# Descending query tiles in the attention stage of a decoder step, with the sample's steps and cached values re-timed

## What is computed

```
y_ssd = rms_norm(y_ssd * silu(z), ssd_norm_g)              # 512 channels, every token

def prompt_attend(...):                                    # query tile i = 128 queries
    idx, valid = index_select(qi, wi, ki, q_pos, k_top)    # decided in an earlier stage
    return sparse_attend(q, k[idx], v[idx], valid)

def sparse_attend(q, ks, vs, valid):                       # 4 heads of 64 channels
    s = where(valid, q @ ks.T * 64**-0.5, -inf)
    return softmax(s) @ vs
```

## Time and profile before

| | us |
|---|---|
| runs | 3554.72, 3562.83, 3569.42; median 3562.83 |
| the profiled execution, whole | 3555.62 |
| its span in the trace | 3553.8 |
| TensorE busy | 3278.0 (92%) |
| attention stage, first and second layer, about | 175 each |

### The profile page before, as it was taken

How to read it: one execution, slowest core, us unless ns; L and a number is a source line. 1 busy time by engine, 2 the same in 40 slices (tenths; PEclk the granted TensorE clock), 3 DMA queues, 4 the chain that set the end, 5 groups by cost and what they waited for, 6 DMA issues and landing times.

```text
span 3553.8 us, 49876 instructions
## 1 busy us (share of the span) xinstructions
PE 3278.0 (92%) x19418; PEld 2659.8 (75%) x19418; DVE 1903.4 (54%) x3006; ACT 1217.4 (34%) x2262; POOL 663.4 (19%) x663
## 2 busy tenths in 40 slices
PE   7899899877999999999999999997788999999997
PEld 4454466545989999999854544765478999999996
DVE  5579783333664434435454996733247544335345
ACT  3256714234242222212233666241434312212123
POOL 0000000011033333334200000001110433334331
PEclk9899999768999999999989999995789999999998
DMA  4111114216011111111111010341340111111111
GB/s 135 45 30 36 34 41 138 87 54 181 8 36 47 35 57 36 48 48 39 64 45 47 30 40 25 97 120 44 116 127 1 45 51 36 51 51 33 57 33 69
DMA packets 168248, 205.77 MB, mean 58 GB/s; under 512 B 61185, under 2 KB 136258, under 8 KB 166850
## 3 DMA queue, kind: packets, MB, share of 16 engines
q1 hardware_dynamic: 163394, 201.43, 18.9%
q10 hardware_dynamic: 4608, 1.05, 0.1%
HBM read 189.33 MB, written 13.08 MB: 57 GB/s over the span
## 4 chain that ended last, share of the span: by engine, by line
PE 69%; DVE 13%; issue 9%; ACT 6%; SPq 1%; DMA 1%; ACTq 0%; POOL 0%; DVEq 0%; POOLq 0%; PEldq 0%
PE PS L785 44%; PE PS L766 5%; DVE MIX L1748 4%; PE PS L798 2%; PE PS L867 2%; ACT X L1388 2%; PE PS L995 1%; PE PS L1168 1%; DVE WORK L1937 1%; SPq L445 1%; PE PS L1145 1%; PE PS L960 1%; PE PS L1155 1%; ACT WORK L1553 1%; PE PS L1183 1%
## 5 line engine op out<-in xcount | busy, mean ns | idle before, releaser
L785 PE MATMUL PS<-WORK_parts,WHIGH_parts 128*128 128x352 f32 x3936 | 806.8, 325 | 19.6 <-DVE MIX_parts L2249 11.2
L785 PEld LDWEIGHTS PS<-WORK_parts,WHIGH_parts 128*128 128x128 f32 x3936 | 669.3, 190 | 23.2 <-issue 23.2
L785 PE MATMUL PS<-WORK_parts,RING_parts 128*128 128x352 f32 x3024 | 655.8, 325 | 0.0
L766 PE MATMUL PS<-X,RING 128*128 128x512 f32 (+1 forms) x1824 | 602.3, 493 | 22.5 <-ACT MIX L1457 9.6
L766 PEld LDWEIGHTS PS<-X,RING 128*128 128x128 f32 x1824 | 303.8, 193 | 321.2 <-issue 319.1
L785 PEld LDWEIGHTS PS<-WORK_parts,RING_parts 128*128 128x128 f32 x3024 | 520.4, 189 | 0.0
L1748 DVE SCALAR_TENSOR_TENSOR WORK<-WORK,VEC 128x1072 f32<-128x1072 f32 (+1 forms) x236 | 483.7, 2050 | 8.4
L509 POOL TENSOR_TENSOR RING_parts<-RING,WHIGH_parts 128x1024 fp32r<-128x1024 f32 (+2 forms) x184 | 373.1, 2028 | 446.5 <-ACT WHIGH_parts L1337 442.0
L1337 ACT ACTIVATE WORK<-PS 128x32 f32<-128x32 f32 (+11 forms) x412 | 190.8, 514 | 732.4 <-PE PS L785 565.2
L785 PE MATMUL PS<-X_parts,WHIGH_parts 128*128 128x352 f32 x2016 | 436.1, 324 | 0.0
L1746 DVE TENSOR_SCALAR WORK<-WORK,VEC 128x1072 f32<-128x1072 f32 (+1 forms) x90 | 70.6, 784 | 515.5 <-ACT WORK L1337 515.5
(11 more groups left out here) (335 smaller groups left out, 4021.4 us busy)
## 6 DMA issues: line engine op xcount, KB each, us to landing
RING<-w_up SPq DMA_DIRECT2D x88, 512.0 KB, 3.5
RING<-cache_k SPq DMA_DIRECT2D x256, 128.0 KB, 2.2
RING<-cache_v SPq DMA_DIRECT2D x256, 128.0 KB, 2.2
RING<-w_in SPq DMA_DIRECT2D x46, 512.0 KB, 3.6
RING<-w_down SPq DMA_DIRECT2D x80, 256.0 KB, 2.6
RING<-cache_kidx SPq DMA_DIRECT2D x192, 32.0 KB, 1.7
WORK<-w_out SPq DMA_DIRECT2D x12, 512.0 KB, 6.3
MIX<-xT SPq DMA_DIRECT2D x3, 1408.0 KB, 9.8
```

The costliest lines, as they stand in the source:

```text
L766: mm = pe.matmul(job_psum(n, w, first=first), stationary(k), moving(k)[:, first:first + w], start=k == 0, stop=k == k_tiles - 1)
L785: mm = pe.matmul(thirds(n)[:, third, :], a, x[:, third * THIRD:(third + 1) * THIRD], start=k == 0 and part == 0, stop=k == tiles - 1 and p ...
```

## The change

`BLOCKS` runs through the query tiles from 7 down to 0, so that the first eight pairs are the long ones. The other jobs get tables of their own: the samples' nine choices at pairs 0 and 1, all ten exponentials at pair 2, the nine transposes at pairs 3 and 4 between the pair's own steps; values from pair 5, two groups a pair up to pair 7 and three from pair 8; squares from pair 8, their sums at pairs 9 to 11, spread and scaling at 12 and 13 (in two parts through banks 3 and 1). A block is turned in pieces of up to four key tiles (`PIECES`), which alternate between banks 4 and 5. TensorE's iteration is now: turn the first block of pair p - 1, `scores(p)`, turn its second block, the other jobs, `weigh(p - 1)`. In the SSD stage the tick that needs bank 2 waits for `ssd["near_decay"]`, which rises after the fourth exponential of the chunk (the "half group").

```diff
-BLOCKS = [(i, h) for i in range(NCHUNK) for h in range(ATT_HEADS)]
-TURNED_AT, WEIGHED_AT = 4, 7
-
-
-def turns_of_pair(p):
-    return range(max(3 * (p - TURNED_AT), 0), min(max(3 * (p - TURNED_AT) + 3, 0), 9))
-
-
-def exps_of_pair(p):
-    return range(max(4 * (p - TURNED_AT + 1), 0), min(max(4 * (p - TURNED_AT + 1) + 4, 0), 2 * QUARTERS + QUADS))
+BLOCKS = [(i, h) for i in reversed(range(NCHUNK)) for h in range(ATT_HEADS)]
+
+
+CHOICES_OF_PAIR = {0: range(0, 5), 1: range(5, 2 * QUARTERS + 1)}
+EXPS_OF_PAIR = {2: range(2 * QUARTERS + QUADS)}
+TURNS_OF_PAIR = {3: range(0, 5), 4: range(5, 2 * QUARTERS + 1)}
+
+
+PIECES = [(_n, _s, min(_s + 4, BLOCKS[_n][0] + 1)) for _n in range(len(BLOCKS)) for _s in range(0, BLOCKS[_n][0] + 1, 4)]
+PIECES_OF = [[_q for _q, _piece in enumerate(PIECES) if _piece[0] == _n] for _n in range(len(BLOCKS))]
+PIECES_TO = [_of[-1] + 1 for _of in PIECES_OF]
 
 
 GATED = [(2 * _q, 2 * _q + 2) for _q in range(NCHUNK // 2)] + [(NCHUNK, NCHUNK + 1)]
-INVERTED_AT = len(GATED) + 1
-assert INVERTED_AT < NCHUNK - 1
+SQUARED_OF_PAIR = {8: (0, 1), 9: (2, 3), 10: (4,)}
+INVERTED_AT = 12
+WEIGHED_AT, VALUE_GROUPS = 5, [2, 2, 2] + [3] * 8 + [2]
+assert sum(VALUE_GROUPS) == STREAM
 
 
 def values_of_pair(p):
-    return range(max(3 * (p - WEIGHED_AT), 0), min(max(3 * (p - WEIGHED_AT) + 3, 0), STREAM))
+    n = p - WEIGHED_AT
+    if not 0 <= n < len(VALUE_GROUPS):
+        return range(0)
+    return range(sum(VALUE_GROUPS[:n]), sum(VALUE_GROUPS[:n + 1]))
...
+                    if q == 0:
+                        pool.wait_ge(att["out"], NCHUNK)
...
                 for n, (i, h) in enumerate(BLOCKS):
-                    if n % 2 == 0 and n // 2 < len(GATED):
-                        square_gated(n // 2)
                     pool.wait_ge(att["inverted"], n + 1)
                     s = SC[n % 4][:, 0:(i + 1) * P]
                     pool.tensor_scalar(s, s, RSUM[:, n:n + 1], 1.0, ALU.mult, ALU.mult).then_inc(att["normed"], 1)
+                    if n % 2:
+                        for q in SQUARED_OF_PAIR.get(n // 2, ()):
+                            square_gated(q)
...
                     if k % 8 == 1:
-                        pe.wait_ge(ssd["decay"], k // 8 + 1)
+                        pe.wait_ge(ssd["near_decay"], k // 8 + 1)
...
                 def scores(p):
 
-                    i, t = divmod(p, 2)
+                    i, t = BLOCKS[2 * p][0], p % 2
                     if p:
                         pe.wait_ge(att["masked"], 2 * p)
-                    if p == NCHUNK:
-                        pe.wait_ge(rms["scaled"], 1)
...
-                def turn_block(n):
-                    i, h = BLOCKS[n]
-                    pe.wait_ge(att["normed"], n + 1)
-                    if n >= 1:
-                        pe.wait_ge(att["copied"], n)
-                    for s in range(i + 1):
-                        mm = pe.transpose(bank(4 + s // 4)[:, (s % 4) * P:(s % 4 + 1) * P],
-                                          SC[n % 4][:, s * P:(s + 1) * P], c("ident"))
+                def turn_piece(q):
+                    n, first, end = PIECES[q]
+                    if first == 0:
+                        pe.wait_ge(att["normed"], n + 1)
+                    if q >= 2:
+                        pe.wait_ge(att["copied"], q - 1)
+                    for key in range(first, end):
+                        mm = pe.transpose(bank(4 + q % 2)[:, (key - first) * P:(key - first + 1) * P],
+                                          SC[n % 4][:, key * P:(key + 1) * P], c("ident"))
                     mm.then_inc(att["turned"], 1)
 
                 def weigh(p):
 
-                    i, t = divmod(p, 2)
-                    pe.wait_ge(att["copied"], 2 * p + 2)
-                    if t == 0 and i >= 1:
-                        pe.wait_ge(att["out_read"], i)
+                    i, t = BLOCKS[2 * p][0], p % 2
+                    pe.wait_ge(att["copied"], PIECES_TO[2 * p + 1])
+                    if t == 0 and p >= 2:
+                        pe.wait_ge(att["out_read"], p // 2)
...
+                    for ch in (4, 5, 6, 7) if again else (0, 1, 2, 3, NCHUNK):
...
-                def sample_steps(p):
-
-                    if 1 <= p <= len(GATED):
-                        yield lambda: sum_squares(p - 1)
-                    if p < TURNED_AT:
-                        for m in range(3 * p, min(3 * p + 3, 9)):
-                            yield lambda m=m: add_choice(m)
-                    for m in turns_of_pair(p):
+                def aside_steps(p):
+
+                    for q in SQUARED_OF_PAIR.get(p - 1, ()):
+                        yield lambda q=q: sum_squares(q)
+                    for m in CHOICES_OF_PAIR.get(p, ()):
+                        yield lambda m=m: add_choice(m)
+                    for m in TURNS_OF_PAIR.get(p, ()):
                         yield lambda m=m: turn_sample(m)
...
                 for p in range(n_pairs + 2):
-                    aside_steps = sample_steps(p)
+                    aside = list(aside_steps(p))
+                    turned = 1 <= p <= n_pairs
+                    if turned:
+                        for q in PIECES_OF[2 * p - 2]:
+                            turn_piece(q)
+                        if p in TURNS_OF_PAIR:
+                            aside.pop(0)()
                     if p < n_pairs:
                         scores(p)
-                    for now in list(aside_steps):
+                        if p in TURNS_OF_PAIR:
+                            aside.pop(0)()
+                    if turned:
+                        for q in PIECES_OF[2 * p - 1]:
+                            turn_piece(q)
+                    for now in aside:
                         now()
-                    if p == NCHUNK + 1:
-                        pe.wait_ge(rms["scaled"], 2)
-                    if 1 <= p <= n_pairs:
-                        turn_block(2 * p - 2)
-                        turn_block(2 * p - 1)
-                    if p == INVERTED_AT:
-                        spread_rstd()
-                    if p >= 2:
-                        weigh(p - 2)
+                    if p in (INVERTED_AT, INVERTED_AT + 1):
+                        spread_rstd(p > INVERTED_AT)
+                    if turned:
+                        weigh(p - 1)
...
+                        if h == 3:
+                            ins.then_inc(ssd["near_decay"], 1)
...
-                def copy_turned(n):
-                    i, h = BLOCKS[n]
-                    keys = (i + 1) * P
-                    act.wait_ge(att["turned"], n + 1)
-                    if n >= 4:
+                def copy_piece(q):
+                    n, first, end = PIECES[q]
+                    act.wait_ge(att["turned"], q + 1)
+                    if n >= 4 and first == 0:
                         act.wait_ge(att["out"], n // 2 - 1)
-                    copy(PROBT[:, h, 0:keys], bank(4, keys)).then_inc(att["copied"], 1)
+                    copy(PROBT[:, BLOCKS[n][1], first * P:end * P], bank(4 + q % 2, (end - first) * P)).then_inc(att["copied"], 1)
...
+                    samples_turned = list(TURNS_OF_PAIR.get(p, ()))
+                    if p >= 1:
+                        for n in (2 * p - 2, 2 * p - 1):
+                            for q in PIECES_OF[n]:
+                                copy_piece(q)
+                            if samples_turned:
+                                copy_sample(samples_turned.pop(0))
                     for n in (2 * p, 2 * p + 1):
                         if n < len(BLOCKS):
                             exp(n)
-                    for m in turns_of_pair(p):
+                            if samples_turned:
+                                copy_sample(samples_turned.pop(0))
+                    for m in samples_turned:
                         copy_sample(m)
-                    if p >= 1:
-                        copy_turned(2 * p - 2)
-                        copy_turned(2 * p - 1)
-                    for m in exps_of_pair(p):
+                    for m in EXPS_OF_PAIR.get(p, ()):
                         exp_sample(m)
-                    if p == len(GATED):
+                    if p == INVERTED_AT - 1:
...
-                for n in range(len(BLOCKS)):
-                    mask(n)
-                    if n % 2:
-                        invert(n - 1)
+                for p in range(len(BLOCKS) // 2):
+                    choices = list(CHOICES_OF_PAIR.get(p, ()))
+                    if p >= 3 and p % 2:
+                        take_out(BLOCKS[2 * p - 6][0])
+                    for n in (2 * p, 2 * p + 1):
+                        mask(n)
+                        if choices:
+                            add_choice(choices.pop(0))
+                    for n in (2 * p, 2 * p + 1):
                         invert(n)
-                    for m in range(3 * (n // 2) + 2 * (n % 2), min(3 * (n // 2) + 2 + n % 2, 9)):
+                        if choices:
```

(20 more changed lines are left out.)

30 lines of the change are left out of this document (17 added, 13 removed).

## The result

The changed kernel takes 3498.7 us (median of four runs, 3495.2 to 3503.6) where the kernel before takes 3561.8 beside it: ratio 0.982, 95% interval 0.981 to 0.984.

A forecast was written before the change was run, and what follows sets the result against it. The prediction took the stream of cached values to set the attention stage's end; attention -8.4 and SSD -4.4 us made -12.8 a layer, -25.6 in both, so 3537 us against a median of 3562.8, range 3514 to 3562.

The forecast's parts named there:

- What bounds the kernel: Attention stage: the stream of cached values sets the end; to gain, it must start earlier or run without holes.
- The stream of values: Attention from the first cached value: 10.7 us of SyncE's slot waits go, 1 and 5 come back; loading 78.2.
- The front: Attention stage up to the first cached value: 81.3 us becomes 77.5, first use 3.7 earlier.
- the wait of 3.96: Pair 3 of attention: TensorE waits about 4 us for ScalarE, which is busy with the samples' exponentials.
- third rival: Attention front: clock rises already in pair 0 and holds; -22.4 us a layer, 3518 in all; chance 0.18.
- 5 at the sums of squares: Pairs 9 and 10 of attention: loss taken as 5 us, between 1 at full clock and about 12 at half.
- second rival: Sums of squares in attention: clock falls and stays down, 12 us instead of 5, 3551 in all; chance 0.24.
- The end: Attention stage, from the last value load to the next stage: left at 10.0 us.
- The SSD stage: SSD stage: waiting for four exponentials instead of nine saves 0.55 us a chunk, -4.4 a layer, between 0 and 9.3.
- The wait that I priced: SSD stage: TensorE waits 1.17 us a chunk for the ninth exponential, 9.3 over eight chunks in the first layer.
- The rule against the change: Values beside short pairs: an engine waiting for loads between bursts falls back to the slow clock; would give 3551.

The follow-up runs named there:

- e5: The changed kernel with values begun one pair later (pair 6) and taken by threes; attention stage 160.1 and 159.9 us.
- e12: The changed kernel with half of the cached value loads left out and every matmul kept; attention stage 137.4 and 139.7 us.
- e16: The kernel before with three quarters of the sums of squares left out; first value at 70.8 and 73.4 us, attention stage 162.3 and 161.0.
- e15: The changed kernel with three quarters of the sums of squares left out; attention stage 150.7 and 151.2 us.
- e6: The changed kernel with each of the five sums of squares done twice; attention stage 167.6 and 169.8 us.
- e7: The changed kernel with matmuls that compute nothing behind the choices, ahead of late value groups and ahead of the last transposes; 3489.0 us, ratio 0.981.
- e4: The changed kernel with the samples' choice spread as in the kernel before and values from pair 7 in threes; 3481.6 us, ratio 0.981.
- e10: The changed kernel with blocks turned and copied whole, as before, instead of in pieces; 3502.8 us, ratio 0.984.
- e9: The kernel before with matmuls that compute nothing added in pairs 0 to 6; 3548.4 us, ratio 0.997.

## Why the prediction was wrong, step by step

**What bounds the kernel: right.** The stream of values sets the end (e5, e12), and it had to start earlier.

**The front: wrong in its size, 14 to 15 us and not 3.7.** This is the step that carried the miss out of the range, 10 to 11 us a layer. Pairs 0 to 4 and the lead of pair 5 were summed as 18 + 17 + 26 (pairs 2 and 3) + 11.5 and 5; in the first layer they took 14.2, 16.2, 24.4, 8.5 and 4.1. The mechanisms were there, the wait of 3.96 among them. In pair 0, 3.8 of the 10, the clock was set too low: I took the lower level for the whole pair and let it rise in pair 1; it was at 0.95 from 686 on, 2.6 us into the stage. Pair 4, 3.0 more, ran at 1.00; its term names no level. Idle time didn't shrink (15.0 before, 14.9 after), so what the front gained is busy time. How the remaining 3 us come about isn't shown. That the clock rises already in pair 0 is the first half of the third rival; its second half, that it holds, did not come. The rival was given 0.18 because choices leave gaps, and the clock did come down among them (0.50 from 694 to 698), but only behind the third choice.

A second reading would have warned me. Taking three quarters of the sums of squares out of the old front, and nothing else, brings 9.1 (e16), so all of them some 12, an estimate by proportion. A gain of 3.7 meant that the long pairs would eat two thirds of that.

**The stream of values: right as a sum, 78.2 against 76.3 and 78.6, by luck in its parts.** Beyond the 72.2 that SyncE needs unhindered, the forecast had 6, of them 5 at the sums of squares; the queue lost 4.1 and 6.4. But with a quarter of the sums it still loses 4.6 and 4.8 (76.8 and 77.0, e15), so it isn't the sums. The loss is spread: the longest group of four takes 3.86 and 4.30 us instead of 2.58. The second rival's mechanism exists: doubled, the sums bring the clock down and cost 15 (e6); as they are, it falls only behind them.

**The end: 10.0 forecast, 8.6 and 8.0 measured.** That less stands behind the last value, with the long pairs gone from it, is argued. A higher clock didn't shorten it (e7).

**The SSD stage: -4.4 forecast, -9.8 and -10.8 measured**, beyond the bound of 9.3 too. The wait that I priced came out about right: TensorE's waits for ScalarE at the turns fall from 9.3 us to 5.8 in the first layer, and its idle time by 2.1 and 2.0. What the sum put at nothing is the granted clock: 7.7 and 8.9 us of busy time went with it in these two executions. This is the second step that failed, 5 to 6 us a layer.

**The rule against the change.** The clock did fall among values beside short pairs: 0.50 in the last window, as the rule says (the Trainium skill, TensorE: Matmul & The Clock Gate, section "HAM oscillation — how this bites in real kernels"). It cost nothing that shows there: at 1.00 the end of the first layer was no shorter (e7).

**The samples' choice in the first pairs** was priced as part of the front's gain; e4 has the same front without it. Of the rest, the moved sums (e16) and the pieces (1 us, e10) are shown to give a part of it; the descending order and the weighing one pair sooner were not tried alone.

How the gain of the front divides exactly stays open: sums (12, estimated), clock (3.6 in e9, with the fills to pay for) and pieces (1) overlap, and the long pairs bring work of their own.

## What to carry to other kernels

When a wait of TensorE goes, price the granted clock of the stretch too: in the SSD stage 2 us less of idle time came with 8 us less of busy time at a higher clock. Read a cause off the sums of the whole stage and not off one chunk: the chunk shown loses a wait for keys, the stage doesn't. Check a sum built up from parts against what is taken out: if 15 us of work leaves the bounding engine and your sum gains 4, name what eats the rest. Try long, solid work around short steps that take turns with another engine (0.94 in e4's front against 0.54); and where a single queue's issue pace sets a stage, a second queue helps only if its engine reaches the issue in time.

## What was not expected of the hardware

- TensorE busy 5.00 of 5.00 us with matmuls of one column, each with its own weight load, is brought down to the lower clock (0.50, e6), where two sums of this kind in a row, 32 matmuls in 3.94 us, ran through at the upper one and it fell behind them (0.66). Being busy didn't keep the clock up.
- Added matmuls that compute nothing made a front shorter: 28.6 us of them, 3.6 us less (e9).
- The same matmuls of the SSD stage took 8 us less of busy time a layer in the changed kernel (137.4 and 137.3 against 145.0 and 146.1), where one wait in each chunk is half a microsecond shorter: the granted clock went from 0.88 and 0.87 to 0.91.
- The same front came between 64.7 and 69.7 us from one execution to another, with the same idle time to 0.1 us; the granted clock was 0.84 in the earliest and 0.77 in the latest.
- A cached page of values costs SyncE's queue 0.65 us of issuing, so 112 of them hold a stretch for 76 us that takes 64 with half of them (e12).
